# Block inverse of the second layer's state recurrence: products over all four quadrants of TensorE, transposed copy turned instead of updated

## What is computed

```python
def step(state, inp):
    r_t, k_t, v_t, w_t, kk_t, a_t = inp
    sa = jnp.einsum('bhvk,bhk->bhv', state, -kk_t)
    state = (state * w_t[:, :, None, :]
             + sa[..., None] * (kk_t * a_t)[:, :, None, :]
             + v_t[..., None] * k_t[:, :, None, :])
    y_t = jnp.einsum('bhvk,bhk->bhv', state, r_t)
    return state, y_t
...
_, y = lax.scan(step, state0, (tm(r), tm(k), tm(v), tm(decay), tm(kk), tm(a)))
```

## Time and profile before

| what | us |
|---|---|
| median of 3 runs | 2128.38 (2127.55 to 2129.3) |
| the profiled execution | 2125.9 |
| its span in the profile | 2124.3 |
| `stage_rwkv` in it, from the first matmul to the end | about 189 |
| setup, 1935.28 to 1964.45 | 29.2 |
| inverse, 1964.45 to 2017.20 | 52.8 |
| two folds, 2017.20 to 2031.27 | 14.1 |

### The profile page before, as it was taken

The page is one execution under the profiler, slowest core; times in us unless marked ns, Lnnn a source line. Parts: engine busy times, 40 slices in busy tenths (PEclk is TensorE's granted clock), DMA queues, the critical chain, the costliest instruction groups (busy, mean ns, idle before and its releaser), DMA issues. The chain is left out here.

```text
span 2124.3 us, 34334 instructions
## 1 busy us (share of the span) xinstructions
PE 1977.8 (93%) x12330; PEld 1583.7 (75%) x12330; DVE 1608.0 (76%) x1778; ACT 1242.6 (58%) x1340; POOL 216.3 (10%) x167
## 2 busy tenths in 40 slices
PE   5997878969999999999999999999999967999997
PEld 2997654558888888888888888888888835777963
DVE  4763432489999999999999999898989855685645
ACT  4331542247777777777777777777777734533221
POOL 0000000001110111010101111110111030160000
PEclk9999876979999999999999999999999978999999
DMA  8772403159999999999999999999999762221011
GB/s 299 246 248 80 173 2 123 40 175 365 393 373 393 378 390 372 386 375 394 376 384 377 389 379 386 377 386 380 383 382 384 302 234 62 70 80 48 4 51 40
DMA packets 139422, 567.14 MB, mean 267 GB/s; under 512 B 16547, under 2 KB 55220, under 8 KB 85396
## 3 DMA queue, kind: packets, MB, share of 16 engines
q1 hardware_dynamic: 126386, 518.94, 64.5%
q0 software_dynamic: 12816, 46.67, 5.8%
q10 hardware_dynamic: 146, 0.48, 0.1%
HBM read 535.64 MB, written 30.41 MB: 266 GB/s over the span
## 5 line engine op out<-in xcount | busy, mean ns | idle before, releaser
L1691 DVE TENSOR_TENSOR w_split<-early,w_split 128x2048 fp32r<-128x2048 f32 x422 | 964.1, 2285 | 18.1 <-ACT w_split L1593 17.9
L1593 ACT ACTIVATE w_split<-early 128x2048 fp32r<-128x2048 f32 x422 | 808.8, 1917 | 272.2 <-PE banks L1560 161.3
L1538 PE MATMUL banks<-w_split,rowsT 128*128 128x512 f32 x3360 | 787.1, 390 | 0.0
L1538 PEld LDWEIGHTS banks<-w_split,rowsT 128*128 128x128 f32 x3360 | 632.6, 188 | 131.5
L1560 PE MATMUL banks<-w_split,hiddenT 128*128 128x512 f32 x1680 | 423.1, 401 | 0.0
L1560 PEld LDWEIGHTS banks<-w_split,hiddenT 128*128 128x128 f32 x1680 | 306.9, 189 | 60.8
L471 PE MATMUL banks<-w_in_hi,hT 128*128 128x256 f32 (+1 forms) x768 | 145.8, 291 | 0.7 <-issue 0.7
L1685 DVE SCALAR_TENSOR_TENSOR hiddenT<-banks,hiddenT 128x256 fp32r<-128x256 f32 x140 | 59.1, 422 | 99.8 <-ACT hiddenT L1609 99.8
L2017 PE MATMUL banks<-h3T,w_in_hi 128*128 128x512 f32 x400 | 128.9, 404 | 1.4 <-DVE h3T L2193 1.4
L471 PEld LDWEIGHTS banks<-w_in_hi,hT 128*128 128x128 f32 x768 | 122.2, 194 | 2.7 <-issue 2.7
L471 PE MATMUL banks<-w_in_lo,hT 128*128 128x256 f32 (+1 forms) x384 | 109.9, 286 | 0.0
(11 more groups left out here) (399 smaller groups left out, 2098.2 us busy)
## 6 DMA issues: line engine op xcount, KB each, us to landing
early<-in_w_gate_up SPq DMA_DIRECT2D x280, 1024.0 KB, 7.1
early<-in_w_down SPq DMA_DIRECT2D x140, 1024.0 KB, 7.5
stage<-in_w_mod SPq DMA_DIRECT2D x24, 1024.0 KB, 5.4
expert_rows<-y_rows POOLq DMA_DIRECT2D x34, 512.0 KB, 8.6
stage<-in_w_in SPq DMA_DIRECT2D x25, 512.0 KB, 3.9
stage<-in_w_in SPq DMA_DIRECT2D x11, 1024.0 KB, 5.5
expert_rows<-cat SPq DMA_DIRECT2D x1, 7680.0 KB
w_out<-in_w_out SPq DMA_DIRECT2D x1, 4096.0 KB, 34.6
```

The costliest lines, as they stand in the source:

```text
L1538: mm = pe.matmul(out, rowsT[:, a, q, :], w[:, part, kk * WIDE:(kk + 1) * WIDE], start=False, stop=(q == KT - 1 and a == 1))
L1593: act.activation(split[:, at, 0, :], raw[s], ACT.Copy).then_inc(high_ready, 1)
L1691: dve.tensor_tensor(split[:, at, 1, :], raw[s], f(split[:, at, 0, :]), ALU.subtract).then_inc(split_ready, 1)
```

## The change

The products of the inverse and of the first fold go over all four quadrants. For that, `solveT`, the intermediate `product` (now viewed as `p`) and `known` are kept with one half of the heads on partitions 0 to 63 and the other on 64 to 127, each with both chunks side by side. `solve` and `level` keep their layout by chunk.

- `spread` (from the layout by chunk to that by half of the heads) makes the intermediate. `gather` (back) makes the update of `solve`. Each is 16 products and takes two banks.
- `solveT` isn't updated at the levels 0 to 3: four 128x128 transposes of `solve` per tile and level (`turn_solve`) and an ACT copy (`copy_solveT`) give it anew, and also ahead of level 0. Only the last level computes its update, with 16 products on two quadrants as before, added by DVE.
- DVE no longer forms the first `solveT` (two operations per tile) nor adds to it at the levels 0 to 3. The level matrices for the next level are made after all four tiles' updates instead of between them.
- In the setup the first of the two `by_chunk` products is a `spread`, and the transposes of alpha put its two halves where `known` wants them; `k.alpha` is laid out by chunk for it.
- The first fold goes over four quadrants; its result is copied half by ACT and half by DVE.
- The masks need no tile of their own: they are loaded in the stage before, over five constants of `k.sq` that are no longer used, and one of the masks is dropped.

```diff
+                sp.dma_start(flat(k.sq[:, KEPT:NSQ, :]), d["tri"].rearrange("p m n -> p (m n)")).then_inc(tri_in, 16)
...
-                sp.dma_start(tri[:], d["tri"]).then_inc(tri_in, 16)
...
+                def turn_solve(t):
+                    for m in range(4):
+                        mm = pe.transpose(k.bank(2 * t)[:, m * P:(m + 1) * P],
+                                          solve[:, t, m].rearrange("p a n -> p (a n)"), k.sq[:, IDENT, :])
+                    mm.then_inc(solveT_ps, 1)
...
+                def spread(n, left, right):
+                    for m in range(4):
+                        for half in range(2):
+                            for side in range(2):
+                                mm = pe.matmul(k.bank(2 * n + side)[halves[half], m * CH:(m + 1) * CH],
+                                               left[halves[side], head(m, half), :], right(halves[side], m, half),
+                                               start=True, stop=True)
+                    return mm
+
+                def gather(t):
+                    for m in range(4):
+                        for half in range(2):
+                            for side in range(2):
+                                mm = pe.matmul(k.bank(2 * t + half)[halves[side], (4 + m) * CH:(5 + m) * CH],
+                                               solveT[halves[half], t, m, side, :],
+                                               p[halves[half], t, side, m, :], start=True, stop=True)
+                    mm.then_inc(x_ps, 1)
...
+                for t in range(NT):
...
+                    pe.wait_ge(solve_ready, t + 1)
+                    turn_solve(t)
                 for s in range(NL):
                     for t in range(NT):
...
+                        pe.wait_ge(solveT_ready, NT * s + t + 1)
                         pe.wait_ge(level_ready, NT * s + t + 1)
                         pe.wait_ge(solve_ready, NT * s + t + 1)
-                        by_chunk(k.bank(2 * t), level, lambda rows, t, h: solve[rows, t, h, :], t
-                                 ).then_inc(p_ps, 1)
+                        spread(t, level[:, t], lambda rows, m, half: solve[rows, t, m, half, :]).then_inc(p_ps, 1)
                     for t in range(NT):
                         pe.wait_ge(p_ready, NT * s + t + 1)
-                        pe.wait_ge(solveT_ready, NT * s + t + 1)
                         if s < NL - 1:
-                            by_chunk(k.bank(2 * t), solveT, lambda rows, t, h: product[rows, t, h, :], t
-                                     ).then_inc(x_ps, 1)
-                        by_chunk(k.bank(2 * t + 1), product, lambda rows, t, h: solveT[rows, t, h, :], t
-                                 ).then_inc(xT_ps, 1)
...
+                            gather(t)
...
+                    if s < NL - 1:
+                        for t in range(NT):
+                            pe.wait_ge(solve_ready, NT * (s + 1) + t + 1)
+                            turn_solve(t)
...
+                def copy_solveT(s, t):
+                    act.wait_ge(solveT_ps, NT * s + t + 1)
+                    act.activation(solveT[:, t].rearrange("p m a n -> p (m a n)"), k.bank(2 * t), ACT.Copy).then_inc(solveT_ready, 1)
```

More of the change, by code:

```diff
@@ L2444, in kind, with alpha_by_half @@
                     mm.then_inc(prod_ps, 1)
+                def turn_solve(t):
[3 more added lines that the diff above has]
+                    mm.then_inc(solveT_ps, 1)
+                def alpha_by_half(t):
+                    for side in range(2):
+                        out = k.bank(4 + side)[:, 4 * CH:8 * CH].rearrange("p (two a n) -> p a two n", two=2, a=2)
+                        for a in range(2):
+                            mm = pe.transpose(out[:, a], k.alpha[:, 2 * t + side, 2 * a:2 * a + 2, :].rearrange(
+                                "p j n -> p (j n)"), k.sq[:, IDENT, :])
+                    mm.then_inc(prod_ps, 1)
@@ L2484, in _ @@
                     pe.wait_ge(act_read, 4 * t + 1)
-                    with_values(4, t, 0)
-                    turn(k.bank(5), features(k.alpha, t)).then_inc(prod_ps, 1)
+                    spread(2, product[:, 2 * (t % 2)],
+                           lambda rows, m, half: heads(k.v_tok[:, t, :])[rows, head(m, half), :])
+                    alpha_by_half(t)
                     pe.wait_ge(dve_read, 4 * t + 3)
@@ new lines, in _ @@
+                    if s < NL - 1:
+                        for t in range(NT):
+                            pe.wait_ge(solve_ready, NT * (s + 1) + t + 1)
+                            turn_solve(t)
+                pairs = lambda ap: ap.rearrange("p (two n) -> p two n", two=2)
+                for t in range(NT):
+                    pe.wait_ge(solveT_last, t + 1)
+                    for m in range(4):
+                        for half in range(2):
+                            for side in range(2):
+                                mm = pe.matmul(by_pair(k.bank(2 * t + half))[halves[side], m % 2, :, m // 2, :],
+                                               solveT[halves[half], t, m, side, :],
+                                               known[halves[half], t, :, side, m, :], start=True, stop=True)
+                    mm.then_inc(solved_ps, 1)
@@ L2511, in fold @@
+                for t in range(NT):
+                    pe.wait_ge(solved_low, t + 1)
+                    pe.wait_ge(solved_high, t + 1)
                     for h in range(HR):
                         for rows in halves:
[L2513 to L2516 removed]
@@ L2518, in _ @@
[L2518 to L2524 removed]
+                            mm = pe.matmul(pairs(k.pp[t][rows, h * P:(h + 1) * P]), out_sa[rows, t, h, :],
+                                           solved[rows, t, :, h, :], start=True, stop=True)
@@ L2632, in _ @@
                         act.wait_ge(p_ps, NT * s + t + 1)
-                        act.activation(product[:, t], heads(k.bank(2 * t)), ACT.Copy).then_inc(p_ready, 1)
+                        act.activation(p[:, t], two_banks(t), ACT.Copy).then_inc(p_ready, 1)
+                    if s < NL - 1:
+                        for t in range(NT):
+                            copy_solveT(s + 1, t)
                 by_head = lambda ap: ap.rearrange("p (h two n) -> p two h n", two=2, n=CH)
@@ L2707, in _ @@
                                                 k.cols[:, GG0 + s:GG0 + s + 1], None, ALU.mult))
+                for t in range(NT):
+                    dve.wait_ge(solved_ps, t + 1)
+                    dve.tensor_copy(half_of(solved[:, t], 1), by_pair(k.bank(2 * t + 1)).rearrange("p a k two n -> p a k (two n)")
+                                    ).then_inc(solved_high, 1)
                 for t in range(NT):
```

153 lines of the change are left out of this document (85 added, 68 removed).

## The result

| what | before | after |
|---|---|---|
| median of the runs, us | 2127.55 (5 runs, 2123.65 to 2129.3) | 2112.84 (5 runs, 2107.69 to 2114.81) |
| ratio after / before | | 0.9929, 95% interval 0.991 to 0.9948 |
| the profiled execution, its span | 2125.9, 2124.3 | 2112.93, 2111.3 |

The kernel is faster by 14.7 us where 25.2 were forecast, and 2112.84 lies above the range, which ended at 2110. I compare the stage from its first matmul on, since that moment moved between 1929.8 and 1939.3 us over the executions of this study although the code ahead of it is the same but for one DMA, where it stands, and the layout of one tile. All distances are read on TensorE from one group's start to the next.

A forecast was written before the change was run, and what follows sets the result against it. PE was taken to bound the inverse, and a loop through DVE and PE after the change; -1.8 - 1.8 - 24.0 + 2.4 = -25.2 us from 2128.4 gave 2103.2 us, range 2099.5 to 2110.

The forecast's parts named there:

- Which part holds the time: Last stage: setup, inverse and first fold get shorter; behind the first fold nothing changes.
- Four quadrants, 0.475 us a group: Spread and gather on PE: 0.475 us per group of 32 instructions instead of 0.93; first fold 3.5 us instead of 7.0.
- Rival 1: New products don't overlap four ways; spreads, gathers and fold keep the old pace: 2121 us; chance 5%.
- The loop through DVE, 6.16 us a level: Inverse: DVE's updates and level matrices, then PE's last spread and first gather, bound each level at 6.16 us.
- The gaps in PE's issue, +2.4: Inverse levels: one gap of 0.5 us in PE's issue at each level, together adding 2.4 us.
- the walk: Operation prices stepped through three engines' order from the setup's last product; second fold starts at 35.8 us instead of 59.8.
- Setup, −1.8 and −1.8: Setup: earlier mask load removes PE's 1.83 us wait (-1.8); one by_chunk group per tile becomes a spread (-1.8).
- Rival 3: More gaps or slower hand-overs: 1.0 us gaps at each level give 2105.7 us, with all terms 2109; chance 17%.
- Rival 4: Gaps in PE's issue hide in waits: 2100.8 us or a little less; chance 12%.
- Rival 2: PE's clock falls to 0.50 from the inverse to the scan; kernel slower, 2145 us; chance 3%.
- The rule on transposes: Skill's rule that transposes don't count as usual PE activity; with 1.8 of 6.2 us per level, rival 2 would come true.
- −24.0: Inverse and first fold: second fold starts 24.0 us earlier, before any gaps in PE's issue.

The follow-up runs named there:

- the run with single instructions: Changed kernel with spread and gather operands in the inverse read as bfloat16, one matmul instruction per product instead of two: 2102.48 us.
- the three kernels with the cheap products: Changed kernel with bfloat16 products in the inverse's spread and gather: issued once (2102.48 us), issued twice (2114.4 us), once with both weight loads moved later (2102.24 us).

## Why the prediction was wrong

- **Which part holds the time.** Right: only the setup, the inverse and the first fold changed; the rest of the stage is within 0.1 us.
- **Four quadrants, 0.475 us a group.** Right: 1.91 us for four groups. The first fold, 3.60 for the forecast 3.5, and the transposes ahead of level 0, 1.9 for 2.0, too. Rival 1 is out.
- **The loop through DVE, 6.16 us a level.** Its size was right, as the run with single instructions shows (6.10, 6.11; the rows had 0.21 us from the end of the issue to DVE's start, where I took 0.22 and 0.05), but it is not what bounds the changed kernel. A level took 7.90, 7.80 and 9.38 us, over the 7.5 that I had named as the point of being wrong.
- **The gaps in PE's issue, +2.4: the step that failed.** I carried the size of a gap (0.46 to 0.75 us) from the setup to the levels, and one gap per level. A gap isn't a price. It is what is left of a block's time when the engine is done with the block before, and so it grows as the work gets denser. What could be carried over is the rate, and it stood in the same rows: the gaps of before end 1945.76, 1952.94 and 1960.40, that is 7.18 and 7.46 us for two blocks (my "7 us and 255 matmuls apart"), 3.66 us a block. A level of 272 instructions is 2.125 blocks, 7.8 us; measured 7.90 and 7.80. The four steps from level to level at 7.8 instead of 6.16 are 6.6 us. The inverse ended 7.2 above the forecast with its 2.4 for gaps, so 9.6 above the walk without them. Of the 3.0 that this leaves, 1.6 are the last measured interval (9.38), which has both the gap of 1.64 and that of 1.36 (1994.89) in it: PE resumed 5.30 us apart there, for 126 instructions. The packet between them began 2.99 us after PE had resumed, where the others in the levels began 1.1 to 1.6 us after. The same 5.30 stand in the changed kernel's second trace and in both kernels that only moved the loads, so 3.7 us are the least time for a block and not a fixed one, and why this packet is late is open. By this estimate the gap of 0.71 ahead of level 0's first update and one of 0.65 in the last products are the rest.
- **Setup, −1.8 and −1.8.** The waits and groups did shrink as said. But the number of PE's instructions in a tile didn't, and 255 of them are two blocks: the setup was already at the rate of its supply, which its gaps said: the step that failed here is that the two terms were taken as if PE had its instructions ready. With the masks alone the setup got no shorter (30.42), and with both terms it came to 28.97. Without the load of 2 MB beside it 26.49 were reached, 2.7 of the 3.6. So part of the loss is the rate, and up to 2.5 us are this load: the 1.89 us gap in the stretch of 342 GB/s, and the granted clock of 0.67 (a stretch at 1.2 of 2.4 GHz) right behind it. How much of the 2.5 is the load's isn't settled, since the same setup code took 28.81 to 31.40 us in five executions with the load at the start and 26.49, 27.44 and 29.19 in three without. What is clear is the first packet of instructions: it began 4.60 to 4.95 us behind the first matmul in all seven executions with the load at the start, and 1.84 to 2.64 in the four without. The kernel before had it at 4.77 too, but there PE stood for 1.83 us of that time waiting for DVE. I had taken this wait away and not asked what the load, which ran beside it, would then run beside.
- **Rivals.** Rival 3, at 2106 to 2109, had the right mechanism and a bound of 1.0 us a gap, once a level; its two measured gaps of about 1.4 us make the difference. Rival 4, gaps that hide, is out. Rival 2 is out for the levels, which stayed at 1.00. The rule on transposes cited with it (Trainium skill, TensorE: Matmul & The Clock Gate, Part 4) is not borne out by them, with 16 transposes in each; in the three kernels with the cheap products the clock did fall around such a row, after fewer or cheaper products with idle time between them, which these runs don't separate.

With the rate in place of the gaps and nothing for the two setup terms, the sum would have been −24.0 + 6.6 = −17.4, or 2111.0, which is 2.7 us more of a gain than the measured 14.7.

## What to carry to other kernels

A gap named issue is the visible end of a supply with a rate of its own: count the matmul instructions between two gaps and the time between their ends, and price a denser stage by that rate, not by the length of the gap. The 3.7 us are the least time for a block here; one can come later. Work that is limited so gets faster only by fewer instructions (one for a product where two were compiled; wider products would be another way, not tried here), not by faster ones or by shorter waits of other engines. A bulk load that is in no hurry belongs beside work that is slow per instruction.

## What the runs showed of the hardware

- TensorE's instructions came in packets of 16 KB, one for 128 matmuls and 128 weight loads, and PE resumed 3.73, 3.81 and 3.73 us apart where it had used them up (5.30 once, see above). It resumed 1.2 to 1.5 us after a packet had landed. At 14.9 ns an instruction 128 of them take 1.9 us, so half of the time is waiting; at 29 ns (3.7 us) the same supply leaves no gap, and the inverse of before showed none.
- In the kernels that issue the load of 2 MB at the stage's start on top of the change, a gap of 1.73 to 2.17 us began 5.3 us behind the first matmul (five executions of four kernels; 1.89 in the changed one). In the three that issue it later on top of the change none stood there, and the first gap came 7.5 us behind the first matmul, with 0.78 to 1.21. In the first fold a load beside it gave 2.01, without it none. Gaps as long (1.79, 1.92, 2.40) came without any load too, so the load is one cause and not the only one.
- Behind the gap of 1.89 us in the setup the granted clock was 0.67 over the next 5 us; behind gaps of 1.4 and 1.6 us in the levels it stayed at 1.00. It was 0.66 over 5 us behind the gap of 2.01 in the first fold of the kernel with the load moved there, and 0.51 over 3.5 us around one of 0.98 in the kernel with single instructions. What decides between the two is open.
- 64x64 products over the same rows but in another order of quadrants went at 19 ns an instruction, between the 15 of all four and the 29 of two opposite ones.
